# A decoder trunk on one core: choices of block 0's heads 2 to 7 later, last two heads' scores in dead rows, group B's rows on ScalarE's queue and normed sooner

## The reference

```python
h = rmsnorm(x, g_norm1) * (1.0 + sc1) + sh1
q, k, v, u, g = jnp.split(h @ w_in, IN_SPLITS, axis=-1)
...
x = x + gt1 * (mix @ w_out)
h2 = rmsnorm(x, g_norm2) * (1.0 + sc2) + sh2
q = (hb @ w_query).reshape(TOK_BLOCK, PEER_HEADS, 2, D_QHALF)
sc = jnp.einsum('thpc,pnc->thpn', q, sub_keys).astype(jnp.float32)
top_s, top_i = lax.top_k(sc, PEER_TOPK)
cand_s = (top_s[:, :, 0, :, None] + top_s[:, :, 1, None, :]).reshape(TOK_BLOCK, PEER_HEADS, kk)
best_s, best_j = lax.top_k(cand_s, PEER_TOPK)
gate = jax.nn.softmax(best_s, axis=-1)
act = jax.nn.gelu(jnp.einsum('thkd,td->thk', expert_u[idx], hb))
return jnp.einsum('thk,thkd->td', (gate * act), expert_v[idx])
```

## Time and profile before

| what | value |
|---|---|
| time, median of 3 runs | 3887.99 us (3885.2 to 3888.14) |
| the profiled execution | 3888.71 us, span 3887.0 us, granted TensorE clock 0.861 of full |
| PE busy | 2866.8 us (74%) |
| DVE busy | 2553.5 us (66%) |
| POOL busy | 1611.2 us (41%) |
| ACT busy | 606.2 us (16%) |
| DMA | 1508.29 MB, mean 388 GB/s |
| of it gathers (software queue) | 1152.39 MB |

### The profile page before, as it was taken

One profiled execution on the slowest core, in us unless ns is written; L12 is line 12 of the kernel. 1 busy time (PEld: TensorE's weight loads), 2 busy tenths in 40 slices (PEclk: granted clock), 3 DMA queues, 4 the chain that ended last, 5 costly groups with the idle time before them and its releaser, 6 DMA issues.

```text
span 3887.0 us, 27071 instructions
## 1 busy us (share of the span) xinstructions
PE 2866.8 (74%) x8298; PEld 1206.8 (31%) x8298; DVE 2553.5 (66%) x3841; ACT 606.2 (16%) x1431; POOL 1611.2 (41%) x1163
## 2 busy tenths in 40 slices
PE   5999997879999966767779788855555555555555
PEld 1333444633334333333323255411111111111110
DVE  3110216695778788555556778899898998777675
ACT  0000201121111122223310011211111111000010
POOL 3000002245433555333334444455655645665553
PEclk6999998989999988888889889977777777777777
DMA  9999547899999999999999999999999999999997
GB/s 313 397 358 364 209 177 275 323 394 412 413 411 411 412 420 410 419 419 419 419 406 403 415 381 412 417 420 420 418 415 409 395 418 420 420 420 420 420 413 301
DMA packets 275010, 1508.29 MB, mean 388 GB/s; under 512 B 27225, under 2 KB 27225, under 8 KB 116777
## 3 DMA queue, kind: packets, MB, share of 16 engines
q0 software_dynamic: 162208, 1152.39, 72.5%
q1 hardware_dynamic: 109538, 336.46, 23.0%
q10 hardware_dynamic: 3120, 17.70, 1.1%
HBM read 1491.81 MB, written 13.80 MB: 387 GB/s over the span
## 4 chain that ended last, share of the span: by engine, by line
DMA 50%; PE 37%; DVE 6%; issue 5%; POOL 1%; ACT 1%; SPq 0%; POOLq 0%; ACTq 0%; DVEq 0%
DMA arena<-in_expert_v_dram,arena 40%; PE ps L921 11%; PE ps L737 7%; PE ps L528 7%; PE ps L687 3%; PE ps L619 3%; DMA arena<-in_w_in_dram 2%; DMA arena<-in_w_out_dram 2%; DMA arena<-in_w_ada_dram 2%; PE ps L516 2%; DMA arena<-in_w_query_dram 1%; POOL arena L2164 1%; DVE arena L1860 1%; PE ps L486 1%; PE ps L730 1%
## 5 line engine op out<-in xcount | busy, mean ns | idle before, releaser
L921 PE MATMUL ps<-arena 128*128 128x512 f32 (+1 forms) x2176 | 1376.6, 771 | 855.3 <-DMA arena<-in_expert_v_dram,arena 837.4
L1912 DVE CUSTOM_DVE_ANT_0 arena<-arena 128x2048 f32<-128x2048 f32 x544 | 1246.1, 2291 | 443.7 <-DMA arena<-in_expert_u_dram,arena 439.0
L2164 POOL DMA_INDIRECT arena<-in_expert_v_dram,arena x544 | 872.2, 1603 | 1072.1 <-PE ps L921 797.5
L921 PEld LDWEIGHTS ps<-arena 128*128 128x128 f32 (+1 forms) x2176 | 450.5, 225 | 1699.1 <-issue 1478.4
L2164 POOL DMA_INDIRECT arena<-in_expert_u_dram,arena x544 | 696.4, 1280 | 637.7 <-DVE arena L1912 381.0
L1860 DVE SCALAR_TENSOR_TENSOR arena<-arena 128x1024 f32<-128x1024 f32 x539 | 691.2, 1282 | 251.4 <-issue 224.5
L737 PE MATMUL ps<-arena 128*128 128x512 f32 x896 | 399.5, 599 | 0.1
L1304 ACT ACTIVATE arena<-arena 128x128 f32<-128x128 f32 (+1 forms) x544 | 204.2, 392 | 1073.2 <-PE ps L921 909.9
L528 PE MATMUL ps<-arena 128*128 128x512 f32 x640 | 290.3, 607 | 8.5 <-DMA arena<-in_w_in_dram 8.5
L737 PEld LDWEIGHTS ps<-arena 128*128 128x128 f32 x896 | 165.6, 190 | 234.9 <-issue 233.9
L687 PE MATMUL ps<-arena 128*128 128x288 f32 (+1 forms) x896 | 218.6, 404 | 18.8 <-DMA arena<-in_w_query_dram 18.8
(11 more groups left out here) (229 smaller groups left out, 1486.8 us busy)
## 6 DMA issues: line engine op xcount, KB each, us to landing
arena<-in_w_ada_dram SPq DMA_DIRECT2D x96, 1024.0 KB, 10.6
arena<-in_w_in_dram SPq DMA_DIRECT2D x80, 1024.0 KB, 8.4
arena<-in_w_query_dram SPq DMA_DIRECT2D x36, 1024.0 KB
arena<-in_w_out_dram SPq DMA_DIRECT2D x32, 1024.0 KB, 5.1
arena<-in_cache_k_dram SPq DMA_DIRECT2D x24, 1024.0 KB
arena<-in_cache_v_dram SPq DMA_DIRECT2D x24, 1024.0 KB
arena<-in_expert_u_dram,arena POOLq DMA_INDIRECT x544
arena<-in_expert_v_dram,arena POOLq DMA_INDIRECT x544
```

The costliest lines, as they stand in the source:

```text
L921: ins = MM(ps[0:rows, c, :], diag[t % 4][:, 0:rows], v_slot[t % RING][:, c * NC:(c + 1) * NC], start=(j == 0), stop=last, skip_group_check ...
L1912: V.tensor_tensor_reduce(out=u_slot[s % RING], in0=u_slot[s % RING], in1=h2[b], scale=1.0, scalar=0.0, op0=ALU.mult, op1=ALU.add, accum_ou ...
L2164: nc.gpsimd.indirect_dma_start(out=slot[s % RING], out_offset=None, in_=table, in_offset=bass.IndirectOffsetOnAxis(ap=idx, axis=0),).then_ ...
```

## The change

- Block 0's choices of heads 2 to 7 are due later: 17.0, 19.6, 23.2, 26.0, 36.0 and 42.0 in place of 12.2, 14.8, 18.4, 21.0, 24.8 and 27.4; that of head 1 one step sooner.
- The scores of block 0's heads 6 and 7 are kept in `sc_last`, in a part of `h2_ta` whose rows the last query unit has read by then, and not in `sc_sb[0]`. ACT's writes to `h_tb` wait for six choices in place of eight; the wait for all eight stands before the mixed rows are written to `mix_tb`, which lies over `sc_last`.
- `x_b` is loaded by ACT, after the turned rows of block 1 and a wait for `norm_h` 4, and not by SP after unit 9.
- `T_NORM1` goes from 13 to 9, `T_TURN1` from 31 to 30, and `T_IN` from 34.8 to 33.8, and with it all that is counted from it.

```diff
--- before.py
+++ after.py
@@ -130,9 +130,9 @@
     return t_qa(p, 3) + 0.6 + 0.5 * i
 
 
-T_NORM1 = 13.0
-T_TURN1 = 31.0
-T_IN = 34.8
+T_NORM1 = 9.0
+T_TURN1 = 30.0
+T_IN = 33.8
 
 
 def t_in(i, q):
@@ -184,7 +184,7 @@
     return t_qb(p, 3) + 0.6 + 0.5 * i
 
 
-TOP_0 = [0, 5.0, 12.2, 14.8, 18.4, 21.0, 24.8, 27.4]
+TOP_0 = [0, 4.0, 17.0, 19.6, 23.2, 26.0, 36.0, 42.0]
 TOP_2 = [t_qb_score(0, 1) + 2.0 + v for v in (0, 4, 12, 17, 24, 31, 38, 45)]
 
 
@@ -320,6 +320,12 @@
         key_f = [at(o + TOPK * i, TOPK) for i in range(2)]; o += 2 * TOPK
         assert o <= DIAG0
         sc_sb = [at(off, PH, 2, NKEY) for off in (HB0, F0, MIX0, MIX0 + D, H20)]
+        sc_last = at(MIX0 + D + NC, 2, 2 * NKEY)
+
+        def scores_of(b, h, j):
+            if b == 0 and h >= 6:
+                return sc_last[:, h - 6, j * NKEY:(j + 1) * NKEY]
+            return sc_sb[b][:, h, j, :]
 
 
         r_slot = [at(R0 + QT * i, 4, NC) for i in range(R_RING)]
@@ -1061,7 +1067,7 @@
                 act.wait_ge(sca_full, h - 1)
                 for j in range(2):
                     for b in range(2):
-                        A.copy(sc_sb[b][:, h, j, :], ps[:, 6 + j, b * NKEY:(b + 1) * NKEY]).then_inc(sca_copied, 1)
+                        A.copy(scores_of(b, h, j), ps[:, 6 + j, b * NKEY:(b + 1) * NKEY]).then_inc(sca_copied, 1)
 
             def gate(b, h):
                 r = ROWS[b]
@@ -1074,6 +1080,9 @@
             first_scores(0)
             gate(0, 0)
             rows_a(1)
+            act.wait_ge(norm_h, 4)
+            for i, b in enumerate((2, 3, SB)):
+                act.dma_start(x_b[i][0:ROWS[b], :], x_of[b]).then_inc(xb_loaded, 16)
             first_scores(1)
 
             def query_a():
@@ -1106,7 +1115,7 @@
                 for b in range(2, BLOCKS):
                     yield t0 + b - 2 + 0.1
                     if b == 2 and name == "hb":
-                        act.wait_ge(idx_ready[0], PH)
+                        act.wait_ge(idx_ready[0], PH - 2)
                     for g in range(4):
                         if name == "hb" and b < NB_P:
                             bank = wait_turn_full(act, (name, b, g))
@@ -1152,6 +1161,7 @@
                 yield T_LN + 5.0
                 act.wait_ge(ln_done, BLOCKS)
                 act.dma_start(sgp, z1[0:NS, 2, :]).then_inc(sgu_stored, 16)
+                act.wait_ge(idx_ready[0], PH)
                 for i in range(2):
                     for b in range(2, BLOCKS):
                         yield t_mix(i, b) + 2.1
@@ -1593,7 +1603,7 @@
 
                 r = slice(0, ROWS[b])
                 pair = range(2)
-                val = [sc_sb[b][r, h, j, :] for j in pair]
+                val = [scores_of(b, h, j)[r, :] for j in pair]
                 for j in pair:
                     n1 = mark(V.max(top_s[r, j, 0:8], val[j]))
                 dv.wait_ge(dve, n1)
@@ -1969,10 +1979,6 @@
             sp.wait_ge(kva_stored, 64)
             for u in range(W_IN):
                 load_w(u, quarter(w_query_v, max(u // 4 - 1, 0), u % 4))
-                if u == 9:
-                    sp.wait_ge(norm_h, 4)
-                    for i, b in enumerate((2, 3, SB)):
-                        sp.dma_start(x_b[i][0:ROWS[b], :], x_of[b]).then_inc(xb_loaded, 16)
             load_in_b(0, 0)
             load_in_b(0, 1)
             load_in_b(0, 2)
```

## The result

The changed kernel takes **3868.47 us** (median, 3865.2 to 3871.61); the kernel before, run beside it, took 3888.06 us (3885.2 to 3890.41). The ratio is 0.9949, with a 95% interval of 0.9938 to 0.9961: 19.8 us faster, between 15.2 and 24.1. The forecast was 3867. The profiled execution took 3869.24 us, with a span of 3867.5 us and a granted TensorE clock of 0.862. Lines have moved by 6 to 10: L921 is now L927, L687 is L693, L1115 is L1124, L1912 is L1922, L1860 is L1870, L2164 is L2170, and the loads of group B's rows are L1085, on ScalarE.

A forecast was written before the change was run, and what follows sets the result against it. From 880 us the span was taken as bytes over rate (412 GB/s), so gains are filled DMA idle time: 1.9 + 9.0 + 7.5 + 3.4 = 21.8 us, 3888.7 - 21.8 = 3866.9, forecast 3867, range 3853 to 3881.

The forecast's parts named there:

- Rival 2: 870 to 1060 us: PE, not DMA, is the bound, so projecting's start counts; 34.6 us gained, 3854; chance 0.08.
- rival 3: Group B's x rows land late on a third queue and DVE stops at step 9; slower, 3896; chance 0.05.
- rival 4: 716 to 806 us: PE keeps its pace, DMA at 376 GB/s, whatever DVE does; 5 us gained, 3884; chance 0.08.
- The rows' move: Group B's row loads go from SP to ScalarE: 1.9 us at 636 to 640, 9.0 at the 704 gap.
- The start's 1.9 us: 636 to 640 us, at 213 GB/s: the row loads begin in this slack and fill it whole; gain 1.9 us.
- The best case: PE's units 8 to 11 never wait for weights: four at 8.1 us from 668.94 end at 701.3.
- The gap's 9.0: 704 to 720 us, at 113 GB/s: of 11.6 us missed 2.6 stay; gain 9.0, bounds 3.6 and 11.6.
- SP's timeline says why: Gap at 704 us: unit 10's load is late because unit 9 and three row loads (2.25 MB) precede it on SP's queue.
- Rival 1: Rows change queues and nothing else, DMA being full at 640 to 704; gap keeps 7 us; 12 us gained, 3877; chance 0.19.
- Normed sooner: DVE's mean squares at steps 9 to 11, scalings 12 to 14: DVE still stops at step 13; frees nothing alone.
- Choices later: 720 to 880 us: two choices leave the DVE-bound stretch and DMA becomes the bound; gain 7.5 us, bounds 3 and 11.2.
- One step sooner: Everything timed by T_IN; POOL's 11.02 us wait at block 2's first choice shrinks; gain 3.4 us, bounds 0 and 4.4.

The follow-up runs named there:

- the gathers held: Kernel before with one wait added: POOL waits until PE has used weight unit 8 before issuing step 12's U gather; 3873.26 us, ratio 0.9966.

## Why the prediction was right, and where it was not

**The bound** was right: bytes over rate from 880 us on, and what was won is DMA idle time filled. Rival 2 (PE is the bound) is out: PE idles 7.7 us in 880 to 1060 and the rate is unchanged. So is rival 3: the rows land in 15.2 us at most. So is rival 4: 720 to 800 moves 411 GB/s, where it had DMA stay at 376 (and PE in 716 to 806 of the kernel before was busy 87.35 of 90 us, not quite without a gap).

**The rows' move, 1.9 + 9.0 us.** The sizes look near and the cause was wrong. The start's 1.9 us: 636 to 640 gained 4 x (358 - 213)/412 = 1.4 us, but 640 to 704 fell from 394 to 382 and lost 1.9. The rows went ahead of unit 7, and PE waits 5.0 us longer for it. (Issuing them took ScalarE 1.7 us, from 638.38 on, and not the 10 it was given.) The best case, four units of 8.1 us from 668.94 to 701.3, met the measured 702 by two errors that cancel: unit 8 began at 674.47, and the four took 27.86 us, 7.0 each. The gap's 9.0: 16 x (406 - 113)/412 = 11.4 us were won there, but the rows' move alone wins 16 x (203 - 113)/412 = 3.5, and 3.2 us in time.

The step that failed is "SP's timeline says why": unit 10's 38.39 us were put down to what stands before it on SP's queue. The larger part was what ran beside it on POOL's: seven gathers of 1 MB issued in 666 to 683 us. Rival 1 had the right rule for this edit, and its price for the gap's rest, 7 us, was near the 8.1 us (16 x (1 - 203/412)) that the run with the rows alone leaves. It is what the Trainium skill says (DMA: Bandwidth & Descriptors, "Issuing engines are not separate DMA queues"), which I gave too little weight: the runs agree with it, since moving a load from one engine's queue to another gave 3.2 us while a change in which transfers are in flight gave 9.0 and 14.7. The same page ("Queues, rings and completion order") says that a DMA engine turns from one queue to another packet by packet. The measured shares, 66% to 36% with the gathers issued ahead and 33% to 70% with them held back, don't contradict that, but no run here tells it from other forms of sharing.

**What closed the gap** was in the diff and not in the prediction: head 1's choice one step sooner. It brings head 1's gate into step 7, where ScalarE is still held by PE's unit 7; DVE waits there (10.54 us alone, 5.98 in the changed kernel), POOL's next U gather waits for DVE, and the weights get through. It is worth 9.0 us alone and 9.0 in the changed kernel, and a wait on POOL does it as well without DVE. The signs that the prediction named came (no load in the chain longer than 20.60 us, the first L927 at 702, L1124 at 820.18, DMA at 411 GB/s, no wait of 11 us at block 2), but none of them could tell the rows' move from this.

**Normed sooner: nothing** was right (3867.1 without it). "DVE still stops at step 13" was not: in the changed kernel it reaches the scaling of step 13 at 705.87, when ScalarE's second root (703.43) is there, since PE's unit 11 was done at 702. With head 1's choice back at 5.0 the stop appears as I described it, 11.8 us. With the rows on SP DVE waits 5.6 us for them at a mean square, but the time shows no cost of it.

**Choices later, 7.5 us (3 to 11.2)**: the mechanism is borne out, the size stays open. DMA is at 411 and 414 GB/s in the two windows, so 80 x 35/412 + 40 x 45/412 = 11.2 us were won there, the upper end. But that contains what the start at 702 in place of 716 brings: with the gathers held and the old choices these stretches miss only 80 x 10/412 + 40 x 28/412 + 40 x 8/412 = 5.4 us. Three pairs of runs with the new choices and with the old ones differ by 2.7 us (all the choices against head 1's alone), 7.4 (all but head 1 against the rows moved) and 7.0 (the same two with the gathers held); the last two have the mean squares and the step shift too, which are worth nothing that can be told. So the edit is worth some 3 to 7 us, and the forecast's "two thirds", which had no row behind it, was rather too much than too little. The choices at steps 36 to 45 cost nothing that a window shows: 880 to 1060 moves 413 GB/s with DVE busy 124.46 of 180.

**One step sooner, 3.4 us**: failed as a gain. POOL's wait at block 2 fell from 11.02 to 4.67 us and 2310 to 2335 went from 343 to 412 GB/s (4.2 us), as forecast. But the other shift that I allowed for took it back: at 2200 to 2240 the kernel after moves 339 GB/s (40 x 73/412 = 7.1 us lost; the kernel before lost 3.5 in 2250 to 2270). The lead in bytes goes 20.9 us at 2200, 16.9 at 2300, 21.3 at 2400. Without the shift POOL's wait is back (11.01 us), the dip is smaller (382 GB/s), and the time is 3869.66: nothing either way that can be told.

In sum 21.8 us were forecast and 19.8 measured. That the number came out is luck: errors met that cancel. The rows' move was credited with 10.9 us and gives 3.2 by itself; head 1's choice, which the prediction left at nothing, gives 9.0; the step shift's 3.4 didn't come. Taken in the order of the runs, the rows' move (3.2), all else but head 1 (7.4) and head 1 (9.0) make the 19.6.

## What to carry to other kernels

A load that takes 38 us where its like take 16 may be late by what is in flight beside it, and not by its own queue: read the bytes of each DMA queue in just that stretch. Gathers issued as far ahead as their slots allow can starve the load that the next work waits for; here one wait on the gathers' engine, placed where they have slack, gave 14.7 us in the kernel before, where the whole change gave 19.6. And every number of a diff is an edit: one that goes against the direction of its neighbours deserves a step of its own.

## What was not expected of the hardware

POOL's indirect gather takes 0.94 to 3.1 us to issue in nearly all rows. In one to three rows of each trace it takes 5.3 to 8.5 us, while DVE runs large operations one right behind the other. POOL's timelines of the kernel after and of the one before:

```profile
2228.05 6.91 POOL L2170 DMA_INDIRECT arena<-in_expert_u_dram,arena  x1 [4.50 <-DVE arena L1922]
```

```profile
2254.28 5.30 POOL L2164 DMA_INDIRECT arena<-in_expert_v_dram,arena  x1 [0.30 <-issue]
```

DVE's timeline of the kernel after: its last operations before its first pause.

```profile
2231.86 2.27 DVE L1922 CUSTOM_DVE_ANT_0 arena<-arena 128x2048 f32<-128x2048 f32 x1
...
2234.92 1.28 DVE L1870 SCALAR_TENSOR_TENSOR arena<-arena 128x1024 f32<-128x1024 f32 x1 [0.78 <-issue]
```

The gather of 2228.05 ends at 2234.96; DVE is busy without a pause from 2202.61 until about 2234.1. The rate falls to 315 and 202 GB/s in 2220 to 2240. The Trainium skill describes such a lock (DMA: Bandwidth & Descriptors, "SWDGE vs HWDGE vs iDMA"): GpSimd writes a gather's descriptors to SBUF, and DVE locks it out there while it runs in its 2-port perf mode. The rows fit a lock, but they don't show whether DVE was in that mode, and no run here took DVE's work away, so the cause isn't shown.
